# Decoder step on one core: the first exponentials behind two copies, their sums behind a gate half, four key scores of the second cache one turn later, and an extraction between gate products

## The reference

```python
x = x + 0.5 * g1 * SwiGLU_1(mod1(rmsnorm(x)))
h = mod2(rmsnorm(x)); [qA|kA|vA|qB|kB|vB|gA|gB] = h @ w_in
#   A: MoBA, 8 heads x 64, blocks of 256 keys, top 3 past blocks + own block
#   B: differential attention, 4 heads, q/k halves of 64, value 128
#   prompt: causal over its 256 tokens; sample: 1024 cached keys per sequence
#           (8 pages of 128, found through page_table) + its own key
x = x + g2 * ((sig(gA) * yA + sig(gB) * yB) @ w_out)
x = x + 0.5 * g3 * SwiGLU_2(mod3(rmsnorm(x)))
```

## Time and profile before

| | us |
|---|---|
| median of 3 runs | 746.17 |
| lowest, highest | 745.51, 746.9 |
| profiled execution, its own time | 747.49 |
| its span, first to last instruction | 745.8 |
| PE busy | 722.3 (97%) |
| DVE busy | 464.2 (62%) |
| ACT busy | 336.8 (45%) |
| POOL busy | 135.7 (18%) |

### The profile page before, as it was taken

How to read it: one execution, slowest core, us unless ns; L and a number is a source line. 1 busy time by engine, 2 the same in 40 slices (tenths; PEclk the granted TensorE clock), 3 DMA queues, 4 the chain that set the end, 5 groups by cost and what they waited for, 6 DMA issues and landing times.

```text
span 745.8 us, 17368 instructions
## 1 busy us (share of the span) xinstructions
PE 722.3 (97%) x6736; PEld 644.8 (86%) x6736; DVE 464.2 (62%) x696; ACT 336.8 (45%) x580; POOL 135.7 (18%) x233
## 2 busy tenths in 40 slices
PE   5899999999999999999989999999999999999998
PEld 2398898999999699999876766789979999999997
DVE  2564545446355779996998665788784555545442
ACT  1463343344254552554255553575564443444441
POOL 0100000002000422597994323210000000000000
PEclk9999999999999999999999999999999999999999
DMA  9977998996996988999999999996626555555531
GB/s 351 378 253 263 314 331 285 317 308 231 413 340 212 385 303 288 354 405 379 407 403 310 405 406 392 337 391 210 207 71 201 188 180 169 179 185 171 187 98 30
DMA packets 116794, 209.57 MB, mean 281 GB/s; under 512 B 6730, under 2 KB 100458, under 8 KB 104434
## 3 DMA queue, kind: packets, MB, share of 16 engines
q1 hardware_dynamic: 107040, 159.46, 61.8%
q0 software_dynamic: 9440, 49.04, 16.7%
q10 hardware_dynamic: 242, 0.11, 0.1%
HBM read 205.33 MB, written 3.24 MB: 280 GB/s over the span
## 4 chain that ended last, share of the span: by engine, by line
PE 76%; DMA 11%; DVE 5%; SPq 3%; issue 3%; ACT 2%; POOL 0%; POOLq 0%; DVEq 0%; ACTq 0%
PE bank L1729 20%; PE bank L1730 19%; PE bank L1731 19%; PE bank L2003 3%; PE bank L1785 3%; DMA early<-in_w_ada 3%; PE bank L2138 3%; DMA raw<-in_ffn_w_down 3%; DVE wlo L1147 2%; DMA raw<-in_w_in 2%; DMA kvA_lent<-in_cache_v_moba 2%; SPq L493 2%; PE bank L2103 1%; PE bank L2104 1%; PE bank L2105 1%
## 5 line engine op out<-in xcount | busy, mean ns | idle before, releaser
L1147 DVE TENSOR_TENSOR wlo<-raw,whi 128x1024 fp32r<-128x1024 f32 (+1 forms) x177 | 208.8, 1199 | 171.0 <-ACT whi L773 168.3
L1729 PE MATMUL bank<-hhi,whi 128*128 128x264 f32 x992 | 285.5, 288 | 2.9 <-POOL wlo L723 1.2
L1730 PE MATMUL bank<-hlo,whi 128*128 128x264 f32 x992 | 281.3, 284 | 0.0
L1731 PE MATMUL bank<-hhi,wlo 128*128 128x264 f32 x992 | 280.9, 283 | 0.0
L773 ACT ACTIVATE whi<-raw 128x1024 fp32r<-128x1024 f32 (+1 forms) x192 | 194.9, 1034 | 105.0 <-PE bank L1731 71.8
L1729 PEld LDWEIGHTS bank<-hhi,whi 128*128 128x128 f32 x992 | 186.8, 188 | 15.5 <-issue 14.3
L1730 PEld LDWEIGHTS bank<-hlo,whi 128*128 128x128 f32 x992 | 187.0, 188 | 0.0
L1731 PEld LDWEIGHTS bank<-hhi,wlo 128*128 128x128 f32 x992 | 186.1, 188 | 0.0
L1729 PE MATMUL bank<-ahi,whi 128*128 128x264 f32 x416 | 118.9, 286 | 1.0 <-DVE alo L1680 0.8
L1731 PE MATMUL bank<-ahi,wlo 128*128 128x264 f32 x416 | 118.2, 284 | 0.0
L1730 PE MATMUL bank<-alo,whi 128*128 128x264 f32 x416 | 117.6, 283 | 0.0
(11 more groups left out here) (305 smaller groups left out, 822.0 us busy)
## 6 DMA issues: line engine op xcount, KB each, us to landing
raw<-in_ffn_w_gate SPq DMA_DIRECT2D x22, 1024.0 KB, 5.4
raw<-in_ffn_w_up SPq DMA_DIRECT2D x22, 1024.0 KB, 5.5
raw<-in_w_ada SPq DMA_DIRECT2D x20, 1024.0 KB, 6.9
raw<-in_w_in SPq DMA_DIRECT2D x20, 1024.0 KB, 11.7
raw<-in_ffn_w_down SPq DMA_DIRECT2D x16, 1024.0 KB, 5.0
kvB<-in_cache_v_diff POOLq DMA_DIRECT2D x44, 256.0 KB, 6.3
kvA<-in_cache_v_moba SPq DMA_DIRECT2D x40, 256.0 KB, 7.6
kvA<-in_cache_k_moba SPq DMA_DIRECT2D x36, 256.0 KB, 6.6
```

What stands on the lines that cost most here:

```text
L1147: dve.tensor_tensor(half_view(wlo[key[1] % 2], key, t), half_view(raw[s], key, t), half_view(whi[key[1] % 2], key, t).bitcast(F32), ALU.su ...
L1729: mm(out, wh, xh, start=start, stop=False)
L1730: mm(out, wh, xl, start=False, stop=False)
L1731: return mm(out, wl, xh, start=False, stop=stop)
```

## The change

Six edits. ACT: `sample_exp(0)` goes from step 14 to step 15, behind two copies and a high half; a one-column exponential stands at its old place, so that the exponential table is loaded there. ACT: the high halves of gate block 2 go behind `turned_probs(0)` and two `pad_weights`. PE: `scores(1, 12)` to `scores(1, 15)` come one turn later, right behind `kv_product(13)` to `kv_product(16)`. PE: `exp_sums(0)` goes behind `kv_product(17)`. PE: `block_sums(1)` goes from ahead of `kv_product(19)` to behind it. PE: the extraction after `c` = 3 goes between the chunks of the second gate half of that turn, two products ahead of each of the chunks 4 to 7, with its two waits at chunk 4. What is computed is the same.

```diff
--- before.py
+++ after.py
@@ -44,6 +44,7 @@
 ADAS = (NMOD * D + ADAW - 1) // ADAW
 KVS = 3
 GUEST_LAST = 8
+LATE_B = 12
 FIRST_LAST = 10
 GATE_GUEST = 18
 BIG = 1e30
@@ -1001,6 +1002,8 @@
                 if 4 <= u + 3 < 20:
                     hi(*filler(u + 3))
                 if u == 14:
+                    nc.scalar.activation(misc[:, 24:25], misc[:, 25:26], ACT.Exp)
+                if u == 15:
                     sample_exp(0)
 
             a.wait_ge(s_krow, 16 * 8)
@@ -1042,12 +1045,12 @@
 
             prompt_exp(0)
             gate_pair(0)
-            for t in range(2):
-                hi(W_GATE + 2, t)
             turned_probs(0)
             a.wait_ge(s_wzero, 1)
             pad_weights(0)
             pad_weights(1)
+            for t in range(2):
+                hi(W_GATE + 2, t)
             gate_pair(1)
             npp = 0
             sample_exp(1)
@@ -2056,6 +2059,8 @@
 
             for u in range(2 * TS + 1):
                 kv_product(u)
+                if u > LATE_B:
+                    scores(1, u - 1)
                 if 1 <= u < 17:
                     kind, i = kv_half(u - 1)
                     if kind == "k":
@@ -2080,7 +2085,7 @@
                     ins.then_inc(s_cur, 1)
                 if u + 2 < 16:
                     scores(0, u + 2)
-                if u < 16:
+                if u < LATE_B:
                     scores(1, u)
                 if u == 11:
                     block_sums(0)
@@ -2089,14 +2094,25 @@
                     pe.wait_ge(s_ncur, 1)
                     pe.wait_ge(s_part, 1)
                     prompt_scores(0)
-                if u == 16:
-                    exp_sums(0)
-
-            def gate_half(s, t):
+
+            def extract(c, f):
+
+                out = bank[:, 7, TS * f:TS * f + 4] if c == 3 else bank[:, 4 + f // 4, TS * (f % 4) + 4:TS * (f % 4) + 8]
+                ins = mm(out, om[:, f // 4, P * (f % 4):P * (f % 4) + P], C("sel4"), start=True, stop=True)
+                if f == KC - 1 or (c > 3 and f == 3):
+                    ins.then_inc(s_ext, 1)
+
+            def gate_half(s, t, c=None):
 
                 pe.wait_ge(s_sig, 2 * s - 2 + t)
                 pe.wait_ge(s_lo, half_done(W_GATE + s, t))
                 for k in range(KC):
+                    if c is not None and k == 4:
+                        pe.wait_ge(s_om, c // 4 + 1)
+                        pe.wait_ge(s_pps, 2 * (c + 1))
+                    if c is not None and k >= 4:
+                        extract(c, 2 * (k - 4))
+                        extract(c, 2 * (k - 4) + 1)
                     wh = whi[s % 2][:, k * 256 + t * P:k * 256 + t * P + P]
                     wl = wlo[s % 2][:, k * 256 + t * P:k * 256 + t * P + P]
                     out = bank[:, 3, GATE_COL:GATE_COL + T]
@@ -2106,10 +2122,11 @@
                 ins.then_inc(s_gemm, 1)
 
             kv_product(17)
+            exp_sums(0)
             kv_product(18)
             turn_probs(0)
+            kv_product(19)
             block_sums(1)
-            kv_product(19)
 
             def o_sum(c):
 
@@ -2176,7 +2193,7 @@
                         pe.wait_ge(s_sig, 1)
                     prompt_scores(c + 1)
                 if gated:
-                    gate_half(c + 1, 1)
+                    gate_half(c + 1, 1, c if c == 3 else None)
                 pe.wait_ge(s_pps, npp)
                 if c:
                     pe.wait_ge(s_pout, c)
@@ -2192,14 +2209,10 @@
                     mm(out[:, 0:TP], vtok[:, 0, v0:v0 + wd], pts[h][:, 0:256], start=True, stop=False)
                     ins = mm(out[:, 128:TP], vtok[:, 1, v0:v0 + wd], pts[h][:, 256:384], start=False, stop=True)
                 ins.then_inc(s_po, 1)
-                if c % 4 == 3:
-
+                if c == KC - 1:
                     pe.wait_ge(s_om, c // 4 + 1)
                     for f in range(KC):
-                        out = bank[:, 7, TS * f:TS * f + 4] if c == 3 else bank[:, 4 + f // 4, TS * (f % 4) + 4:TS * (f % 4) + 8]
-                        ins = mm(out, om[:, f // 4, P * (f % 4):P * (f % 4) + P], C("sel4"), start=True, stop=True)
-                        if f == KC - 1 or (c > 3 and f == 3):
-                            ins.then_inc(s_ext, 1)
+                        extract(c, f)
             o_sum(KC - 1)
             pe.wait_ge(s_sig, 14)
 
```

## The result

The changed kernel takes 750.84 us in the median of 9 runs (749.42 to 754.39), the kernel before 746.17 (745.31 to 746.9, 9 runs on the same chip). The ratio is 1.0072, its 95% interval 1.0056 to 1.0089. It is slower, as forecast, but by 4.7 us and not by 2.5, and it lies 0.3 us above the upper end of the range. Its profiled execution took 749.42, the lowest of the nine.

The account below looks back on a forecast made before the run. PE, with hardly a gap, was taken as the bound: what makes it wait or slows its clock counts. 747.49 + 2.6 (sums) + 1.5 (clock) - 1.55 (extraction) = 750.0, or 748.7 us on the median's scale; range 745.7 to 750.5.

Parts of the forecast that it names:

- ACT and the 1.79 us: Middle stage: later `sample_exp(0)` removes PE's 1.79 us gap ahead of `v_turn(15)` and POOL's 1.41 us wait; high half 18 near 378.
- The later scores and POOL: Middle stage: late scores hold POOL's loads, product 18 starts at 389.4 instead of 388.98; gain of 1.79 + 1.20 us gone.
- Block sums: Second group: `block_sums(1)` behind product 19 starts a 6.4 us chain; PE waits 2.6 us at `exp_sums(1)`, sums 2.6 us later.
- Where product 19 ends: Middle stage on PE: product 19 ends at 396.65, from product 18's start at 389.4 plus 7.49 less 0.25 us.
- rival (c): Middle stage: POOL not held, product 18 starts when PE is free, DVE limits the gain; 743.7 us, chance 0.06.
- The clock: Behind the new gap at `exp_sums(1)`: the granted clock falls, costing 1.5 us, between bounds of nothing and 1.55 us.
- the sign that the prediction named: Changed kernel's trace: a granted clock below 1.00 behind a PE gap of 2 us or more ahead of `exp_sums(1)`.
- rival (a): At `exp_sums(1)`: the wait comes but the clock holds behind it; 747.2 us, no measurable change, chance 0.22.
- The extraction: Turn 3: extraction between gate chunks keeps the clock up, minus 1.55 us; other bound nothing.

Follow-up runs that it names:

- both back: Changed kernel with `scores(1, 12)` to `scores(1, 15)` and `block_sums(1)` in their old places: ratio 1.0002, 746.56 us.
- two idle matmuls: Changed kernel with two unread matmuls of 512 columns in the gap ahead of `exp_sums(1)`: ratio 1.0039, 749.41 us.
- `block_sums(1)` alone: Kernel before with only `block_sums(1)` moved behind product 19: ratio 1.0031, 749.07 us.
- first two late: Changed kernel with only `scores(1, 12)` and `scores(1, 13)` one turn later, `scores(1, 14)` and `scores(1, 15)` in their old turns: ratio 1.0065, 752.05 us.
- other gaps filled: Changed kernel with two unread matmuls ahead of the prompt scores and one ahead of product 18, the gap at `exp_sums(1)` open: ratio 1.0056, 750.8 us.
- the last two late, again: Second measurement of the changed kernel with only `scores(1, 14)` and `scores(1, 15)` one turn later: ratio 1.0035, 748.46 us.
- repeat: Changed kernel measured once more, unaltered, against the kernel before: ratio 1.0081, 751.51 us.
- the scores back: Changed kernel with `scores(1, 12)` to `scores(1, 15)` back in their old turns: ratio 1.0011, 747.46 us.
- the first run with the last two late: First measurement of the changed kernel with only `scores(1, 14)` and `scores(1, 15)` one turn later: ratio 1.0037, 748.18 us.
- the extraction alone: Kernel before with only the extraction moved inside the gate half: ratio 0.9999, 746.57 us.
- the late scores alone: Kernel before with only `scores(1, 12)` to `scores(1, 15)` one turn later: ratio 1.0036, 749.49 us.
- two filled versions: Changed kernel with unread matmuls: two ahead of `exp_sums(1)` (749.41 us), or two ahead of the prompt scores and one ahead of product 18 (750.8 us).
- `block_sums(1)` back: Changed kernel with `block_sums(1)` back ahead of product 19: ratio 1.0036, 749.1 us.
- 5 idle matmuls: Changed kernel with five unread matmuls of 512 columns in the gap ahead of `exp_sums(1)`: ratio 1.0073, 752.11 us.
- sums behind prompt scores: Changed kernel with `exp_sums(1)` behind the prompt's turned probabilities and the prompt scores: ratio 1.0058, 750.58 us.

## Why the prediction was right or wrong

**ACT and the 1.79 us: right.** No gap is left ahead of `v_turn(15)`, and high half 18 came at 379.34, 1.3 us behind the "near 378" and early enough. The table load and the small exponential lay in idle time. What this gives is taken by what is late next: with both back the time is that of before, with the waits of 1.33, 1.06 and 1.05 us shown there.

**The later scores and POOL: right in time, incomplete in cause.** The load of use 16 began at 371.58 (372.2 forecast) and low half 18 ended at 389.17 (389.0 to 389.5); product 18 started at 389.31 (389.4). That it fits so well is partly luck: the load began 0.6 us early, but POOL then needed 14.79 us (371.58 to 386.37) and not 14.01 to the end of the load of use 18, with the wait of 0.88 us for `scores(1, 14)` in it, and low half 18 took 2.78 us where up to 3.28 was allowed. And the step followed POOL alone. The scores also made DVE late (last keys 376.08 for 373.52) and opened two gaps that it did not have, 1.97 us at the prompt scores and 1.06 at product 17. It took "the gain is gone" for their whole effect, where alone they cost 2.7 us.

**Block sums: right.** The chain from `block_sums(1)` to the sums is 404.28 - 397.93 = 6.35 us (6.4), the wait 2.49 (2.6); alone the edit costs 2.3 us.

**Where product 19 ends: this step failed by 0.9 to 1.3 us.** "Product 19 now ends at 396.65" took product 18's start and added what PE had needed before. `block_sums(1)` came at 397.93 behind a clock fall, and at 397.56 in the execution without one (two idle matmuls), where `turn_probs(0)` waits 1.27 us for DVE. The forecast's rival (c) names DVE's full queue as the limit for a gain, but its lateness was not carried into the forecast itself. In that execution two small operations of DVE take 3.12 us (L1458) and 2.58 us (L1495) between 380.90 and 389.01, where each took 0.16 in others; DVE has no gap from there to the turned probabilities, so by estimate either of them alone is longer than the wait of 1.27.

**The clock: the price right, how often it is paid wrong.** The sum had +1.5 for one fall behind the new gap and -1.55 for the extraction, together nothing. A fall behind the sums does cost 1.4 us. But of the eight profiles with the wait of 2.48 or 2.49 us ahead of `exp_sums(1)` only four show one there: `block_sums(1)` alone, first two late and other gaps filled 0.8 to 1.5 us behind the start of the sums, the last two late, again, from 0.45 us ahead of it. The changed kernel, its repeat, the scores back and the first run with the last two late show none there. So the sign that the prediction named, a clock below 1.00 behind the gap, is not met in the changed kernel's own profile. The falls of the changed kernel's two profiles lie behind shorter gaps instead: 389.69 behind that of 1.73 us, and in the repeat 374.47 and 391.53 behind those of 1.77 and 1.75. And in the profile of the extraction alone the clock falls at 384.30, at the end of a wait of 2.31 us ahead of `v_turn(15)`, the gap that stayed at full clock in the earlier trace rows. That one gap in one execution was what spoke for rival (a). The Trainium skill, "TensorE: Matmul & The Clock Gate", section "HAM oscillation", describes waits that bring the clock down again and again; here that agrees in part, with a mean clock of 0.993 against 0.997 but no fall behind four of the eight waits of 2.48 or 2.49 us.

**The extraction: this step failed.** "Minus 1.55 us" is 0.9999, with an interval of -1.0 to +0.8 us. The row that it rested on is one execution. Of the three profiles with the extraction in its old place only that one has a fall at turn 3 (the others are `block_sums(1)` alone and the late scores alone), and of the 24 executions of the kernel before that were measured beside this run five show a clock of 1.000, so no fall at all. The price was right again: from the start of this extraction to that of turn 7 pass 46.13 us with the fall and 44.48 in both profiles without. The forecast took these 1.55 us off the median, 746.17, when only the profiled execution, 747.49, is known to have had them to give back. On the scale of that execution its own sum was 750.0.

**The whole, split by executions.** The five executions of the kernel before at 1.000, just named, have a median of 745.79. The changed kernel has none, but its two filled versions have five (748.80, 749.02, 749.17, 749.20, 749.41), with its order of useful work: 749.17. The difference of 3.4 us is the waiting, and the sums of the two idle matmuls' profile agree with it (403.90 for 400.46). The forecast had 2.6: 0.8 short, by DVE. The rest is clock by subtraction. From there to the medians are 0.8 us for the kernel before (746.57) and 1.7 for the changed one (750.84), 2.3 in the repeat (751.51), so 0.9 to 1.6 us more, where the forecast had -0.05. This is a split of the measured loss and no test of it, since the parts add up by the way they are taken, and the medians come from different chips. By it the forecast's 2.1 us too few are 0.8 us of waiting for DVE and the rest clock. The 1.55 us of the extraction are most of that: without them the forecast would have been 746.17 + 2.6 + 1.5 = 750.3.

## What to carry to other kernels

A gain read at the place of an edit must be followed to every engine whose buffers the moved work frees: here four scores one turn later held POOL's queue and DVE's keys, and moved POOL's work beside small operations of DVE that then had to wait. One profiled execution shows which clock falls are possible, not how often they come; a clock term belongs in a sum only with its share among the executions, and the list of their granted clocks tells that. Two idle matmuls that fill a gap are a cheap test of what the gap costs beyond its length.

## What was not expected

**A small DVE operation can wait for POOL.** In the changed kernel's rows above, L1458 runs from 381.72 to 384.19 and POOL's four operations from 381.39 to 384.17; L1495 from 386.62 to 389.19, POOL's from 386.39 to 389.17; L1369 from 368.05 to 370.38, POOL's from 367.51 to 370.32. All three are operations of two inputs from SBUF. In the repeat with the last two late L1369 starts at 368.10 and takes 0.48 us, POOL's end at 368.53. It does not always last to POOL's end: the next L1495 of the changed kernel, at 390.66, takes 0.16 us while POOL works from 389.33 to 392.13, and with the scores back L1458 ends at 383.43 after 1.62 us where POOL works from 381.96 to 384.75. The Trainium skill, "SBUF — State Buffer", section "SBUF: two separate sides", says that DVE and GpSimd share one pair of ports as an exclusive lock, held for a whole instruction; the rows agree that the two exclude each other, but three times DVE waited out four instructions of 0.7 us each, so that L1495 took 2.4 us more than its 0.16.

The three operations take 7.4 us of DVE together. L1369 is what opens the gap of 1.97 us ahead of the prompt scores, the longest new one behind that of 2.49: in the kernel before POOL's four operations ran there from 366.24 to 369.04 and the same operation (L1366) took 0.50 us; now they start at 367.51, behind the wait of 1.67 us for `scores(1, 12)`. So a part of what the late scores cost is this. No run takes the holds away by themselves, so their price in time is not shown.

**The clock falls later too.** The profiles of six variants (`block_sums(1)` back, 5 idle matmuls, other gaps filled, sums behind prompt scores, last two late again, first two late) are down at 492 to 495 as well, behind the extraction of turn 7, which no edit touches. It costs 0.5 us: from that extraction to the last instruction pass 257.1 to 257.2 us in the six and 256.6 in the changed kernel's. A slower middle stage is not enough for it, as the repeat and the late scores alone reach turn 7 as late (492.62 and 493.27) and keep the clock. I have no run that tells why it is met only in those six.
